# First layer of a twin-network kernel: tables on 48 partitions, early issues and bias bands from SyncE, shared modulation products

## The chip, the cores and the metric

One core of a Trainium2 chip. The metric is the device time of one execution in microseconds, the median of 3 runs. All arithmetic is in float32; large products are made of three passes on split operands (below).

## The reference, cut to what matters

Two networks run one after the other on a 512 x 1024 activation. The first has two layers, the second four. Only the first layer matters here: a modulation computed from a conditioning vector c, then a dilated-window attention with 18 heads in three groups, whose logits take a bias from a table of 32 buckets.

```
mod = silu(c) @ ada_w[i] + ada_b[i]               # 3 x 1024 values: shift, scale, gate
u = x * (1 + scale) + shift
q, k, v, gate = split(u @ w_in)                   # 18 heads of 64, groups with dilation 1, 4, 16
s = q k^T / 8 + bias_table[t5_bucket(offset)]     # only |offset| <= window / 2
o = softmax(s) v, weighted over the groups by softmax of log-sum-exp
y = (o * silu(gate)) @ w_out
x = layernorm(alpha * x + mod_gate * y)
```

The second network's third mixer is a differential attention with 4 heads that needs a bias table of its own (`rel_bias_2`) and a scalar lambda, from exponentials of two products of vectors.

## The kernel before

**Layout.** Activations are held transposed: 8 slices (KD) of 128 channels on partitions by 512 tokens. Weights come as a stream of chunks of 128 x 1024 (512 KB) through a ring of four slots, `w_raw`. Each chunk is split: ScalarE (ACT) copies it to `w_hi` in fp32r (`split_hi`, line 394, which waits for the landing and for the slot's last use by TensorE), GpSimd (POOL) makes `w_lo` as the difference (line 489), and SyncE (SP) loads the next chunk into a slot when `w_lo` of the old one is done (`four`, line 459). TensorE (PE) then makes each product in three matmuls (`product`, lines 401 to 403): hi x hi, hi x lo, lo x hi.

**Order.** Every engine has its program written out by hand; semaphores tie them. SP issues x slice 0, four chunks, seven x slices, and from then on only chunks, each behind its wait. ACT's queue issues everything else, in line with ACT's own work: the columns, the modulation blocks (`ada_ring`, four slots of 1 MB), the tables, the late rows (`late_ring`, three slots), the bias bands. A wait or a DMA issue on a sequencer holds all that is behind it there.

**Tables.** `hot` (67 rows x 3072) and `tab` (67 x 22) stand on 67 partitions: 32 buckets of the dilated bias, 3 rows for the windows' masks, 32 buckets of the second network's bias. PE multiplies them (lines 503 and 510), ACT copies the results to `bias_sb` (lines 1110 and 1117) and stores them to DRAM. From there `spread_a` (line 1155) writes 32 copies of each head's row to DRAM, six heads at a time, and `load_bands_a` (line 1163) reads skewed pieces back as `band_a`, 24 transfers for each of two heads. `bias_rows` (line 1234) are the same for the second network.

**Modulation.** For each of 8 steps t VectorE (DVE) sums the eight products of a 128 x 256 block with silu(c) (`ada_rows`, lines 1537 to 1548), PE sums over the partitions with a column of ones (line 553), DVE adds the base (line 1571) and forms the modulated slice `tmp` (line 1553), ACT rounds it to `u_hi` (line 1143), DVE subtracts to `u_lo` (line 1559). PE then runs the slice against the first four chunks (lines 556 to 565): 12 matmuls per slice. This is called the opening.

**Attention.** Three pairs of heads (jp = 0, 1, 2), two heads in each of three groups. Per pair: six projections q and k (`a_project`, line 567; in pair 0 the first four are the opening, and q and k of group 0 of the next pair are made in units 6 and 7 of the pair before), values (`a_values`, line 577), three gates, and eight units of scores, maxima, exp, turn and product. A projection is read by ACT (`a_parts`, line 1181: `qa_hi` or `ka_hi`) and DVE (line 1624: `qa_lo` or `ka_lo`). PE's values wait for all three `q_evac` of the pair. Pair jp uses 13 chunks: 6 for q and k, 4 for the values, 3 for the gates.

**Late rows.** The rest of the modulation (gate of layer one, all of layer two) is 32 rows of 128 x 1024, r = c // 8 the part: DVE takes two in each `a_parts` (line 1635, `late_rows`), ACT refills the ring in its own `a_parts`, ahead of the read of the projection (line 1185).

The waits of ACT in its `a_parts`:

```
chunk("a_in", at)
for c in (2 * e + 1, 2 * e + 2):
    if LATE_SLOTS <= c < LATE:
        act.wait_ge(late_used, c - LATE_SLOTS + 1)
        act.dma_start(late_ring[:, c % LATE_SLOTS, :], ada_late[c])
act.wait_ge(chunk_used, BASE["a_in"] + at + 1)
```

## Time and profile before

| | us |
|---|---|
| median of 3 runs | 3165.66 (3165.46 to 3169.13) |
| the profiled execution | 3166.86 |
| its span | 3165.1 |
| PE busy | 2855.0 (90%) |
| DVE busy | 1534.1 (48%) |
| POOL busy | 1123.4 (35%) |
| ACT busy | 917.7 (29%) |

DMA queue q1 (SP's) moved 241.20 MB, q10 (ACT's) 42.31 MB, of 285.14 MB in all. The profile lists for each instruction its start, its duration, and in brackets the idle time of its engine before it with what ended that. A name with a q behind it (ACTq, SPq) is the engine's own queue issuing; the time shown there is the time that the issues took, waits between them included. A matmul's duration reaches past the start of the next one, so the pace of a run of matmuls is read from the distance of starts. A float32 matmul shows as two passes (x4 for two calls), an fp32r one as one.

### The profile page before, as it was taken

The page shows a single profiled execution, that of the slowest core. Times are in us where ns is not written, and L with a number is a line of the kernel's source. Part 1 is how long each engine was busy: PE and PEld are TensorE (multiplying, and loading weights), DVE is VectorE, ACT ScalarE, POOL GpSimd, SP SyncE. Part 2 cuts the span into 40 slices and gives each one's busy share as a digit, 9 for nine tenths or more (in the row PEclk, how much of TensorE's full clock was granted, in tenths as well). Part 3 has the DMA queues.
Part 4 walks back from the last instruction along what each step waited for, and adds up shares of the span by engine and source line. Part 5 has one row for each costly group of instructions (what it writes and reads, how often), then busy time and mean ns, then how long its engine had stood idle before and what let it go on. Part 6 is the DMA issues. An engine that isn't in the chain of part 4 may idle for free.

```text
span 3165.1 us, 35456 instructions
## 1 busy us (share of the span) xinstructions
PE 2855.0 (90%) x13184; PEld 2325.8 (73%) x13184; DVE 1534.1 (48%) x2019; ACT 917.7 (29%) x1261; POOL 1123.4 (35%) x461
## 2 busy tenths in 40 slices
PE   1598897999899899997999988987999989899997
PEld 0487685878678688886788867875888868778885
DVE  2543435688666454305644125755644046464412
ACT  1132232455322322224322223333222231232222
POOL 1133222410234254441344433212544434434443
PEclk9899998999999999998999999998999999999998
DMA  5445321310122233332232322211333323223332
GB/s 194 123 162 160 99 64 60 100 34 21 60 73 88 65 106 99 98 102 85 75 98 93 103 83 72 72 41 54 109 97 100 100 69 98 93 73 94 99 100 87
DMA packets 106126, 285.14 MB, mean 90 GB/s; under 512 B 38658, under 2 KB 38786, under 8 KB 104664
## 3 DMA queue, kind: packets, MB, share of 16 engines
q1 hardware_dynamic: 67392, 241.20, 24.4%
q10 hardware_dynamic: 38619, 42.31, 4.4%
q8 instruction: 83, 1.36, 0.2%
q14 instruction: 32, 0.26, 0.0%
HBM read 281.22 MB, written 8.85 MB: 92 GB/s over the span
## 4 chain that ended last, share of the span: by engine, by line
issue 63%; POOL 23%; PE 11%; another core or an unknown queue 2%; POOLq 1%; DVE 1%; ACT 0%; ACTq 0%; DVEq 0%
POOL w_lo L489 23%; PE ps L401 4%; PE ps L402 4%; PE ps L403 4%; POOLq L488 0%; POOLq L162 0%; PE ps L503 0%; DVE x L1936 0%; DVE tmp L1930 0%; DVE rs L440 0%; ACT bias_sb L1110 0%; PE ps L432 0%; ACT w_hi L394 0%; DVE y L1979 0%
## 5 line engine op out<-in xcount | busy, mean ns | idle before, releaser
L489 POOL TENSOR_TENSOR w_lo<-w_raw,w_hi 128x1024 fp32r<-128x1024 f32 x452 | 1122.5, 2488 | 2027.2 <-ACT w_hi L394 2027.0
L401 PE MATMUL ps<-u_hi,w_hi 128*128 128x512 f32 x2240 | 909.8, 406 | 108.5 <-DVE u_lo L1768 58.2
L402 PE MATMUL ps<-u_lo,w_hi 128*128 128x512 f32 x2240 | 883.6, 394 | 0.0
L403 PE MATMUL ps<-u_hi,w_lo 128*128 128x512 f32 x2240 | 882.8, 394 | 0.0
L394 ACT ACTIVATE w_hi<-w_raw 128x1024 fp32r<-128x1024 f32 x452 | 474.2, 1054 | 869.6 <-PE ps L403 789.7
L401 PEld LDWEIGHTS ps<-u_hi,w_hi 128*128 128x128 f32 x2240 | 427.7, 191 | 220.4 <-DVE u_lo L1768 65.4
L402 PEld LDWEIGHTS ps<-u_lo,w_hi 128*128 128x128 f32 x2240 | 428.3, 191 | 99.0 <-issue 12.0
L403 PEld LDWEIGHTS ps<-u_hi,w_lo 128*128 128x128 f32 x2240 | 427.5, 191 | 90.9
L401 PE MATMUL ps<-h_hi,w_hi 128*128 128x512 f32 x704 | 278.1, 395 | 0.0
L403 PE MATMUL ps<-h_hi,w_lo 128*128 128x512 f32 x704 | 278.1, 395 | 0.0
L402 PE MATMUL ps<-h_lo,w_hi 128*128 128x512 f32 x704 | 278.1, 395 | 0.0
L1961 DVE TENSOR_TENSOR tmp<-ps,rs_x 128x512 f32<-128x512 f32 x88 | 60.8, 691 | 352.5 <-PE ps L403 352.5
L1979 DVE COPY y<-ps 128x512 f32<-128x512 f32 x32 | 22.1, 692 | 413.1 <-PE ps L403 413.1
L1598 DVE CAST h_hi<-tmp 128x512 f32 (+1 forms) x88 | 194.9, 2215 | 11.7 <-DVE tmp L1963 9.6
L1408 ACT ACTIVATE tmp<-tmp 128x512 f32<-128x512 f32 x88 | 55.6, 632 | 423.4 <-DVE tmp L1959 423.4
L403 PEld LDWEIGHTS ps<-h_hi,w_lo 128*128 128x128 f32 x704 | 132.0, 187 | 32.4
L401 PEld LDWEIGHTS ps<-h_hi,w_hi 128*128 128x128 f32 x704 | 132.0, 187 | 32.3
L402 PEld LDWEIGHTS ps<-h_lo,w_hi 128*128 128x128 f32 x704 | 132.0, 187 | 32.2
L401 PE MATMUL ps<-w_hi,u_hi 128*128 128x256 f32 (+1 forms) x256 | 82.5, 322 | 50.7 <-DVE qa_lo L1632 49.3
L401 PE MATMUL ps<-m_hi,w_hi 128*128 128x512 f32 x256 | 103.5, 404 | 12.1 <-DVE m_lo L2121 12.1
L402 PE MATMUL ps<-m_lo,w_hi 128*128 128x512 f32 x256 | 102.8, 402 | 0.0
L403 PE MATMUL ps<-m_hi,w_lo 128*128 128x512 f32 x256 | 102.6, 401 | 0.0
(262 smaller groups left out, 3312.8 us busy)
## 6 DMA issues: line engine op xcount, KB each, us to landing
w_raw<-in_stream SPq DMA_DIRECT2D x452, 512.0 KB, 3.5
late_ring<-in_ada_late ACTq DMA_DIRECT2D x32, 512.0 KB, 4.5
ada_ring<-in_ada ACTq DMA_DIRECT2D x8, 1024.0 KB, 7.6
dilated_bias_rows<-dilated_bias ACTq DMA_DIRECT2D x18, 244.1 KB, 5.1
band_a<-dilated_bias_rows ACTq DMA_DIRECT2D x96, 28.0 KB, 2.0
x<-in_x SPq DMA_DIRECT2D x8, 256.0 KB, 10.3
bias_rows<-bias_scratch ACTq DMA_DIRECT2D x4, 512.0 KB, 9.0
out_yT<-x SPq DMA_DIRECT2D x8, 256.0 KB, 2.0
```

The source lines that it names most:

```text
L394: nc.scalar.activation(w_hi[:, slot, :], w_raw[:, slot, :], ACT.Copy).then_inc(hi_ready, 1)
L401: nc.tensor.matmul(o, w[0], v[0], start=start, stop=False)
L402: nc.tensor.matmul(o, w[0], v[1], start=False, stop=False)
L403: return nc.tensor.matmul(o, w[1], v[0], start=False, stop=stop)
L489: nc.gpsimd.tensor_tensor(w_lo[:, s, :], w_raw[:, s, :], w_hi[:, s, :].bitcast(F32), ALU.subtract).then_inc(lo_ready, 1)
L1408: nc.scalar.activation(tmp[:, f, :], tmp[:, f, :], ACT.Silu).then_inc(g_silu, 1)
L1598: ch(nc.vector.tensor_copy(hi, src))
L1961: ch(nc.vector.tensor_tensor(tmp[:, 2 + f, :], bank(at + 1), rs_x[:, :], ALU.mult))
L1979: nc.vector.tensor_copy(y[:, m, :], bank(DOWN_BANKS[j])).then_inc(out_evac, 1)
```

## The change

- The tables stand on 48 partitions: the second network's buckets share rows 0 to 31 with the first's, in other columns.
- SP issues the modulation blocks, between the x slices, and the 48 band transfers of each pair, after rounds 3, 5 and 8 of four chunks. ACT's band and block issues go.
- Of the eight products per step DVE makes five; PE makes the other three as matmuls of the block itself with columns of silu(c), summed in PSUM with the column sum.
- In the opening ACT makes both the rounded and the plain modulated slice (`tmp`), from x, with scale and bias; DVE only subtracts.
- The second network's table and the lambda sum are multiplied after the opening, not before; the projections wait for their copies.
- ACT issues all 18 spreads after the opening; the copy of the second table and the exp for lambda come after them.
- The late rows: two at each `a_parts` except those of group 0 in the later pairs, four more ahead of the first maxima of each pair. ACT's refills stand behind the read of the projection, and behind the first two value chunks.

```diff
-BIAS_K = 32 + NG + 32
+BIAS_K = 48
+BANDS_AFTER = (3, 5, 8)
+ADA_PE = 3
@@ SP
+            def load_ada(t):
+                slot = t % ADA_SLOTS
+                if t >= ADA_SLOTS:
+                    sp.wait_ge(ada_turned, t - ADA_SLOTS + 1)
+                sp.dma_start(ada_ring[:, slot, :, :], ada_w[t]).then_inc(ada_landed[slot], 16)
+            def load_bands(jp):
+                sp.wait_ge(a_rows[jp], 16 * 2 * NG)
+                if jp:
+                    sp.wait_ge(m_ready, UNITS * jp)
+                for hh in range(2):
+                    for b in range(QB):
...
             load_x(0)
+            load_ada(0)
...
             four(0)
             for t in range(1, KD):
+                load_ada(t)
                 load_x(t)
-            with sp.Fori(1, N_CHUNKS // RING) as i:
+            done = 1
+            for jp in range(NJ):
+                with sp.Fori(done, BANDS_AFTER[jp]) as i:
+                    four(i)
+                done = BANDS_AFTER[jp]
+                load_bands(jp)
+            with sp.Fori(done, N_CHUNKS // RING) as i:
                 four(i)
@@ PE
-            pe.wait_ge(lam_prod, 1)
             pe.wait_ge(bias_copied, 1)
...
+            pe.wait_ge(c_silu, 1)
@@ PE, the opening
                 if t < KD:
+                    slot = t % ADA_SLOTS
+                    pe.wait_ge(ada_landed[slot], 16 * (t // ADA_SLOTS + 1))
                     pe.wait_ge(ada_used, t + 1)
                     for c in range(2):
-                        mm = pe.matmul(bank(7 - t % 2, 1, at=480 + c), ada_acc[:, t % 2, c * P:(c + 1) * P],
-                                       ones[:, 0:1], start=True, stop=True)
+                        w, o = slice(c * P, (c + 1) * P), bank(7 - t % 2, 1, at=480 + c)
+                        for k in range(KD - ADA_PE, KD):
+                            pe.matmul(o, ada_ring[:, slot, k, w], sc[:, k:k + 1], start=k == KD - ADA_PE, stop=False)
+                        mm = pe.matmul(o, ada_acc[:, t % 2, w], ones[:, 0:1], start=False, stop=True)
                     mm.then_inc(ada_turned, 1)
@@ PE, after the opening
+            pe.wait_ge(ada_turned, KD)
+            pe.wait_ge(lam_prod, 1)
+            for j in range(2):
+                at = A_BIAS_AT + j * S
+                mm = pe.matmul(bank(4 + j, p1=HC), tab[0:BIAS_K, HA:NB], hot[0:BIAS_K, at:at + S], start=True, stop=True)
+            mm.then_inc(bias_done, 1)
+            pe.matmul(bank(7, 2), ones[:, :], col[:, 16:18], start=True, stop=True).then_inc(lam_sum, 1)
@@ PE, a_project and a_values
-                    pe.wait_ge(ada_turned, KD)
+                    pe.wait_ge(bias_copied, 2)
...
+                pe.wait_ge(lam_exp, 1)
@@ ACT, the start: silu, split_hi(0), table copy, split_hi(1), split_hi(2); then
             begin("a_in")
             for t in range(KD):
-                if t + ADA_SLOTS < KD:
-                    act.wait_ge(ada_used, t + 1)
-                    act.dma_start(ada_ring[:, t, :, :], ada_w[t + ADA_SLOTS]).then_inc(ada_landed[t], 16)
-                act.wait_ge(u_tmp, n.up("u_tmp"))
-                nc.scalar.activation(u_hi[:, t, :], tmp[:, t % 2, :], ACT.Copy).then_inc(u_hi_ready, 1)
+                act.wait_ge(mod0_ready, t + 1)
+                act.wait_ge(x_landed[t], 16)
+                if t >= 2:
+                    act.wait_ge(u_ready, t - 1)
+                for dst in (u_hi[:, t, :], tmp[:, t % 2, :]):
+                    nc.scalar.activation(dst, x[:, t, :], ACT.Identity, scale=mod[:, 8 + t:9 + t],
+                                         bias=mod[:, t:t + 1]).then_inc(u_hi_ready, 1)
+                if t == 1:
+                    act.dma_start(a_bias_dram, bias_sb[0:HA, 0:A_BIAS]).then_inc(bias_stored, 16)
+                if t == 4:
+                    for c in range(LATE_SLOTS):
+                        act.dma_start(late_ring[:, c, :], ada_late[c]).then_inc(late_landed[c], 16)
+            act.wait_ge(bias_stored, 16)
+            for jp in range(NJ):
+                spread_a(jp)
+            act.wait_ge(bias_done, 2)
+            nc.scalar.activation(bias_sb[0:HC, A_BIAS_AT:], ...)
+            act.wait_ge(bias_copied, 2)
+            act.dma_start(bias_dram, bias_sb[0:HC, A_BIAS_AT:]).then_inc(bias_stored, 16)
+            act.wait_ge(lam_sum, 1)
+            nc.scalar.activation(col[:, 18:20], bank(7, 2), ACT.Exp).then_inc(lam_exp, 1)
@@ ACT, a_parts
-                for c in (2 * e + 1, 2 * e + 2):
...
                 ins.then_inc(a_hi_ready, 1)
+                if jp == 0 or g:
+                    late_refills(2)
+
+            def late_refills(count):
+                for _ in range(count):
+                    c = n.up("late")
+                    if c <= LATE - LATE_SLOTS:
+                        slot = (c - 1) % LATE_SLOTS
+                        act.wait_ge(late_used, c)
+                        act.dma_start(late_ring[:, slot, :], ada_late[c - 1 + LATE_SLOTS]).then_inc(late_landed[slot], 16)
@@ ACT, the pairs
-                    if g == 1:
-                        for hh in range(2):
-                            load_bands_a(jp, hh)
-                    if g == 2 and jp + 1 < NJ:
-                        spread_a(jp + 1)
                     if jp == 0 and g == 2:
+                        act.wait_ge(bias_stored, 32)
...
                 for c in range(QB):
                     chunk("a_in", A_CH * jp + 2 * NG + c)
+                    if c < 2:
+                        late_refills(2)
@@ DVE
-                for k in range(1, KD):
+                for k in range(1, KD - ADA_PE):
...
+            def first_lo(t):
+                dve.wait_ge(u_hi_ready, n.up("u_hi", 2))
+                nc.vector.tensor_tensor(u_lo[:, t, :], tmp[:, t % 2, :], u_hi[:, t, :].bitcast(F32),
+                                        ALU.subtract).then_inc(u_ready, 1)
...
-                    ch(nc.vector.tensor_tensor(pair, bank(7 - k % 2, 2, at=480), ada_base[:, :, k], ALU.add))
-                    dve.wait_ge(x_landed[k], 16)
-                    modulated(k, 0)
+                    nc.vector.tensor_tensor(pair, bank(7 - k % 2, 2, at=480), ada_base[:, :, k],
+                                            ALU.add).then_inc(mod0_ready, 1)
...
+                    if r >= 2:
+                        dve.wait_ge(late_turned, r - 1)
...
-                for c in (2 * e, 2 * e + 1):
+                if jp == 0 or g:
+                    more_rows(2)
...
+                more_rows(4)
                 if jp == 1:
                     late_mod(1)
                 a_maxima(i0)
```

## Rows read from the trace of the kernel before

**Rows 1.** The page, its first line.

```profile
span 3165.1 us, 35456 instructions
```

**Rows 2.** Windows: stretch, length, busy time of each engine, PE clock, DMA share, GB/s.

```profile
480.00:3165.00 2685.00, 2512.00 (x11424) 2035.60 (x11422) 1340.47 (x1648) 792.72 (x1082) 1010.07 (x408) 0.97 0.27 83
```

**Rows 3.** Time line of the start: start, duration, engine and line, what, idle before.

```profile
2.25 2.17 ACTq L1102 DMA_DIRECT2D hot<-in_onehot  x1
...
53.27 6.67 PE L503 MATMUL ps<-hot,tab 67*18 67x512 f32 x8 [53.27 <-DMA hot<-in_onehot]
...
59.98 1.79 ACT L1110 ACTIVATE bias_sb<-ps 18x1953 f32<-18x1953 f32 x1 [20.81 <-PE ps L503]
```

**Rows 4.** Windows of the first 53 us, while `hot` is on its way.

```profile
5.00:20.00 15.00, 0.00 (x0) 0.00 (x0) 0.68 (x3) 0.00 (x0) 0.00 (x0) 1.00 1.03 397
...
40.00:53.00 13.00, 0.00 (x0) 0.00 (x0) 3.05 (x7) 0.00 (x0) 0.00 (x0) 1.00 0.07 28
```

**Rows 5.** Time line of PE in the opening, first and second slice.

```profile
76.85 0.80 PE L401 MATMUL ps<-u_hi,w_hi 128*128 128x512 f32 x1 [9.14 <-DVE u_lo L1559]
...
82.14 0.85 PE L553 MATMUL ps<-ones,ada_acc 128*128 128x1 f32 x4
...
82.84 0.57 PE L401 MATMUL ps<-u_hi,w_hi 128*128 128x512 f32 x1
...
85.76 0.51 PE L553 MATMUL ps<-ones,ada_acc 128*128 128x1 f32 x4
```

**Rows 6.** Time line of DVE and ACT in the opening.

```profile
84.06 3.61 DVE L1546 SCALAR_TENSOR_TENSOR ada_acc<-ada_ring,sc,ada_acc 128x256 f32<-128x256 f32 x7
...
87.58 0.69 DVE L1559 TENSOR_TENSOR u_lo<-tmp,u_hi 128x512 fp32r<-128x512 f32 x1
...
94.12 0.63 ACT L1143 ACTIVATE u_hi<-tmp 128x512 fp32r<-128x512 f32 x1 [4.53 <-DVE tmp L1553]
```

**Rows 7.** Time line of PE: two of the four blocks of late columns.

```profile
179.67 1.95 PE L612 MATMUL ps<-ones,late_acc 128*128 128x1 f32 x16
...
412.66 2.25 PE L612 MATMUL ps<-ones,late_acc 128*128 128x1 f32 x16
```

**Rows 8.** Time line of PE: the opening's last matmul, and the four stalls.

```profile
112.33 0.39 PE L403 MATMUL ps<-u_hi,w_lo 128*128 128x512 f32 x1
...
127.03 0.80 PE L401 MATMUL ps<-u_hi,w_hi 128*128 128x512 f32 x1 [14.32 <-DVE qa_lo L1632]
...
158.34 0.69 PE L401 MATMUL ps<-w_hi,u_hi 128*128 128x384 f32 x1 [18.36 <-DVE qa_lo L1632]
...
277.72 0.69 PE L401 MATMUL ps<-w_hi,u_hi 128*128 128x384 f32 x1 [15.57 <-DVE qa_lo L1632]
...
392.01 0.69 PE L401 MATMUL ps<-w_hi,u_hi 128*128 128x384 f32 x1 [15.36 <-DVE qa_lo L1632]
```

**Rows 9.** Time line of ACT and DVE between the opening and the values.

```profile
110.34 3.17 ACTq L1161 DMA_DIRECT2D dilated_bias_rows<-dilated_bias  x5
...
119.31 0.60 ACT L1192 ACTIVATE ka_hi<-ps 128x512 fp32r<-128x512 f32 x1 [4.21 <-DVE late_acc L1610]
...
125.58 0.60 ACT L1194 ACTIVATE qa_hi<-ps 128x512 fp32r<-128x512 f32 x1 [4.73 <-DVE late_acc L1610]
...
133.20 2.60 DVE L1610 SCALAR_TENSOR_TENSOR late_acc<-late_ring,sc,late_acc 128x1024 f32<-128x1024 f32 x2
```

**Rows 10.** Time line of ACT: the first of pair 0's band issues, and ACT's next instruction.

```profile
131.92 2.15 ACTq L1173 DMA_DIRECT2D band_a<-dilated_bias_rows  x4
...
156.02 1.06 ACT L394 ACTIVATE w_hi<-w_raw 128x1024 fp32r<-128x1024 f32 x1 [23.52 <-issue]
```

**Rows 11.** The page, POOL's costliest group: line, count, busy, mean ns, idle before.

```profile
L489 POOL TENSOR_TENSOR w_lo<-w_raw,w_hi 128x1024 fp32r<-128x1024 f32 x452 | 1122.5, 2488 | 2027.2 <-ACT w_hi L394 2027.0
```

**Rows 12.** Time line of PE and DVE: pair 0's second scores, and its eighth maximum.

```profile
188.73 0.49 PE L401 MATMUL ps<-ka_hi,qa_hi 64*128 64x512 f32 x1
...
222.70 0.15 DVE L1661 TENSOR_REDUCE col<-col 128x1 f32<-128x2 f32 x1
```

More of the change, by code:

```diff
@@ L456, in load_x @@
                 sp.dma_start(x[:, t, :], xT[:, t, :]).then_inc(x_landed[t], 16)
+            def load_ada(t):
[9 more added lines that the diff above has]
+                    for b in range(QB):
+                        r = slice(32 * b, 32 * b + 32)
+                        for b2 in range(QB):
+                            at = (2 * jp + hh) * 32 * A_BIAS + (4 * (b2 - b) + 12) * SPAN + 31
+                            src = bass.AP(a_bias_rows.tensor, at, [[A_BIAS - 1, 32], [SPAN, 7], [1, 32]])
+                            dst = band_a[r, hh, 0:7 * P].rearrange("p (d c) -> p d c", d=7)[:, :, 32 * b2:32 * b2 + 32]
+                            sp.dma_start(dst, src).then_inc(band_landed, 16)
+                        for g in (1, 2):
+                            at = (HPG * g + 2 * jp + hh) * 32 * A_BIAS + (15 - 4 * b) * SPAN + 31
+                            src = bass.AP(a_bias_rows.tensor, at, [[A_BIAS - 1, 32], [4 * SPAN, QB], [1, 32]])
+                            w = slice((6 + g) * P, (7 + g) * P)
+                            dst = band_a[r, hh, w].rearrange("p (d c) -> p d c", d=QB)
+                            sp.dma_start(dst, src).then_inc(band_landed, 16)
             load_x(0)
+            load_ada(0)
             def four(i):
@@ L505, in _ @@
             mm.then_inc(bias_done, 1)
-            pe.wait_ge(lam_prod, 1)
             pe.wait_ge(bias_copied, 1)
-            for j in range(2):
-                at = A_BIAS_AT + j * S
-                mm = pe.matmul(bank(4 + j, p1=HC), tab[0:BIAS_K, HA:NB], hot[0:BIAS_K, at:at + S], start=True, stop=True)
-            mm.then_inc(bias_done, 1)
-            pe.matmul(bank(6, 2), ones[:, :], col[:, 16:18], start=True, stop=True).then_inc(lam_sum, 1)
+            pe.wait_ge(c_silu, 1)
             def turn(o, src):
@@ L1111, in _ @@
                                  ACT.Copy).then_inc(bias_copied, 1)
-            act.wait_ge(bias_copied, 1)
-            act.dma_start(a_bias_dram, bias_sb[0:HA, 0:A_BIAS]).then_inc(bias_stored, 16)
-            for c in range(RING - 1):
+            for c in range(1, RING - 1):
                 split_hi(act, c)
-            act.wait_ge(bias_done, 2)
-            nc.scalar.activation(bias_sb[0:HC, A_BIAS_AT:], ps[0:HC, 4:6, :].rearrange("p a b -> p (a b)"),
-                                 ACT.Copy).then_inc(bias_copied, 1)
             begun = set()
@@ L1161, in spread_a @@
                         act.dma_start(a_bias_rows[head], src).then_inc(a_rows[jp], 16)
[L1163 to L1179 removed]
+            begin("a_in")
@@ new lines, in _ @@
+            for t in range(KD):
+                act.wait_ge(mod0_ready, t + 1)
[10 more added lines that the diff above has]
+                        act.dma_start(late_ring[:, c, :], ada_late[c]).then_inc(late_landed[c], 16)
@@ L1565, in _ @@
                 if t >= 2:
-                    modulated_lo(t - 2)
+                    first_lo(t - 2)
                 if t:
@@ L1634, in a_parts, with more_rows @@
                                                    op1=ALU.subtract).then_inc(q_evac, 1)
-                for c in (2 * e, 2 * e + 1):
+                if jp == 0 or g:
+                    more_rows(2)
+            def more_rows(count):
+                for _ in range(count):
+                    c = n.up("late") - 1
                     if c < LATE:
@@ L2220, in _constants @@
     hot = np.zeros((BIAS_K, A_BIAS_AT + BIAS_W), np.float32)
-    hot[32 + NG + _buckets(delta, 128), A_BIAS_AT + np.arange(BIAS_W)] = 1.0
+    hot[_buckets(delta, 128), A_BIAS_AT + np.arange(BIAS_W)] = 1.0
     delta = ((np.arange(31) - 15)[:, None] + 16 * (np.arange(SPAN) - 31)[None, :]).reshape(-1)
@@ L2342 @@
         table[32 + g, g * HPG:(g + 1) * HPG] = 1.0
-    table[32 + NG:, HA:] = a["rel_bias_2"]
+    table[0:32, HA:] = a["rel_bias_2"]
     hot, rope, inv, windows = _constants()
```

46 lines of the change are left out of this document (9 added, 37 removed).

## The prediction

> **What bounds the kernel now.** I read the page first, then the windows by stage, then what TensorE (PE) waits for, and last the time lines of the engines before each of its waits. The span is 3165.1 us [rows 1]. From 480 us on PE is busy 2512 of 2685 us and the change touches nothing there [rows 2]; so all of it is decided in the first layer, before 480 us, where PE's idle time is a delay of everything behind it.
>
> At the start PE's first matmul waits 53.27 us for the table `hot`, issued at 2.25 us [rows 3]. Look at the transfers meanwhile: 397 GB/s from 5 to 20 us, but 28 GB/s at a DMA share of 0.07 from 40 to 53 us, about one engine of sixteen [rows 4]. Then the table's matmuls take 6.67 us and their copy 1.79 us [rows 3], and the opening (8 slices of the modulated input, 12 matmuls each) begins at 76.85 us [rows 5] and ends at 112.33 + 0.39 = 112.7 us [rows 8]. A slice comes every 4.53 + 0.63 = 5.16 us, paced by VectorE's eight products [rows 6].
>
> After it PE stands still four times [rows 8]: 14.32 us to 127.03, 18.36 to 158.34, 15.57 to 277.72, 15.36 to 392.01. All four end with `qa_lo`. The first is the pace of the units of ScalarE (ACT) and VectorE, 125.58 - 119.31 = 6.27 us each, ACT waiting for late rows [rows 9]. The other three are 48 band transfers that ACT issues in front of its own work, 131.92 to 156.0 us, 23.52 us of idle ACT, so 0.5 us each [rows 10].
>
> **The change, part by part.** All times are made against the profiled run, 3166.9 us, 1.2 above the median of 3165.7.
>
> *Tables on 48 partitions.* The row shows one engine's rate for 67 partitions [rows 4]. At 397 GB/s the table's 0.59 MB share the engines with 1.25 MB of x and first modulation block; both are in after about 1.9/0.397 = 5 us plus 2 to 4 us of start: `hot` at 7.5, the block at 9. The bound on the other side is no gain in engines (rival 2). The Trainium skill, DMA: Bandwidth & Descriptors, section Why a DMA increments its semaphore by 16 and not by 1, has a transfer use the largest number of engines up to 16 that divides its outer sizes: 1 for 67, 16 for 48. By that rule the forecast stands, without it rival 2.
>
> *Start.* Table matmuls 7.5 to 14.2, copy to 16.0 [rows 3]. ACT's silu no longer stands behind its ring issues. On SP the blocks go ahead: x0, block 0, four chunks, then three pairs of block and x, 7 MB, in by about 22 us at 397 GB/s. Column sums of slice 0 at 16.1, 16 small matmuls where there were 4: 0.85 x 4 = 3.4 us at the low clock [rows 5], so to 19.8. The first modulated slice needs VectorE's pair, two ACT passes and a subtraction, and PE must do columns 1: its 12 matmuls start about 23.5. w_lo of the first chunks (2.49 us each on POOL, [rows 11]) is ready about 24, so it just follows.
>
> *Opening.* VectorE per slice: five products instead of eight, 3.61/7 = 0.52 each, so 1.5 us less, and the modulating pass goes to ACT: about 3.3 us. ACT does two passes of 0.63 [rows 6]; the form with scale and bias from columns is not in the trace, bounded by 0.6 and 1.0 us (and a table load once), covered by the 4.9 below either way. PE per slice: 82.84 to 85.76 = 2.9 us for 12 matmuls at 2.4 GHz [rows 5], plus 16 small ones, 1.95 us [rows 7]: 4.9 us. PE becomes the bound, and the slice is hardly shorter than 5.16. So sharing the products gives little by itself. First slice at 1.2 GHz 76.85 to 82.14 = 5.3 us [rows 5]: 23.5 + 5.3 = 28.8; then 6 x 1.95 + 7 x 2.9 = 32; one fall of the clock as in this opening, 2 us: end at 63. Blocks 4 to 7 wait on SP for sums that are one slice old; 1 MB needs 3 to 5 us, hidden by four slots. **Gain 112.7 - 63 = 49.7.**
>
> *From the opening to the values.* Here something is added: after its last slice (59) ACT issues 18 spreads instead of 6, 3.17/5 = 0.63 each [rows 9] = 11.3, to 70.5; copy of the second table, table load and exp about 2.5 together (an estimate from the 1.79 of the first copy [rows 3]): 73. These 18 move 4.4 MB; if the queue holds ACT up they cost up to 20 instead of 11. Only then come the units that let PE go on, and PE's second table (four matmuls where the first took eight) hides beneath. A unit is now split 1.05, high part 0.6, low part 0.7 [rows 6, 9], two late rows 2.60 [rows 9], an issue 0.35: 5.3; the refills are issued before the split, so the landing is nearly covered (6.27 if not: +1 per unit). `qa_lo` of the second group comes at 73 + 12 = 85, where it came 14.3 after the opening and now comes 22: ACT's burst costs 8 here. Two projections of 13 us together (127.03 to 140.0 [rows 8]): values start at 98. With bands off ACT the next `qa_lo` is there by 96. Before: 158.34 - 112.7 = 45.6; now 35. **Gain 10.4.**
>
> *Bands on SP, pair 0.* SP issues 48 bands at 0.5 us once chunk 11 is issued (chunk 7 split, about 97): 97 to 121. Queued behind: chunk 12, landed about 125, and ACT waits for it in order before it copies the values, 127. PE has work: values to 118, scores, late columns 1.95 and a gate projection until 128.4 (158.34 to 188.73 is 30.4 [rows 8, 12]). So it hides, with 1 to 2 us to spare. The values lose the restart at the low clock: **gain 1.9**, a small wait for chunk 9 kept.
>
> *Pair 1.* SP waits for the eighth maximum (222.7 in old time [rows 12]), issues to 247, chunk 20 lands 251; ACT wants it at about 256, after the projection before the last. The stall of 15.57 goes, and 1.7 of restart (384-column matmuls at 0.17). **Gain 17.3.** *Pair 2.* The same, 392.01 - 277.72 = 114.3 later and a little more: bands 339 to 363, chunk 32 at 367. ACT wants it three projections of 5.4 before 376.65, at 361. ACT is 6 us late, its unit by 3, and PE is still in the projection before. Next late is nothing. **Gain 15.36 + 2.4 = 17.8.** The two halves of the late rows moved out of units 6 and 7, and the four extra before the maxima, lie under some 18 us of values: nothing, and if that cover went, 4 x 1.3.
>
> Sum: 49.7 + 10.4 + 1.9 + 17.3 + 17.8 = 97.1; 3166.9 - 97.1 = **3070 us**, 3.0% less. Its own range is 3058 to 3084: below, no fall of the clock and shorter waits in the first 20 us; above, units of 6.27 (+3), spreads held up (+9).
>
> **Rival 1: the opening runs at 1.2 GHz.** Of four blocks of 16 small matmuls one runs 2.25 us and ahead of slow matmuls, the one at 179.67 not [rows 7]; every slice now has such a block. For it: the clock was low for the first slice. Against: gaps now nearly vanish, and the fast slices before had gaps of 2 us. Price: 6 x 3.4 + 7 x 5.3 = 57.5 for 32 + 2, so +23: 3093. The Trainium skill, TensorE: Matmul & The Clock Gate, section What's actually happening, says that "activity releases the throttle"; by it this rival hangs on whether single-column matmuls are activity, which no row settles.
>
> **Rival 2: the table's transfer stays on one engine.** 0.59 MB at 28 GB/s is 21 us, beside that engine's sixteenth of 8 MB, 18 us: `hot` at 40. The opening slides by 32 less the 2 to 3 waited for blocks: +30, 3100.
>
> **Rival 3, slower: SP chokes on the bands.** SP carries all weights, and each pass of 48 stands before a chunk. If SP gets them off only as they land (2 us instead of 0.5), each pass is 96 us, PE starves three times: 3 x 48 x 1.5 = 216, less 10 of slack, 3276. It decides above 0.5 + (97 + 10)/144 = 1.24 us per issue. Against it: ACT issued the same shapes at 0.5 [rows 10], and nothing makes SP's issue dearer. A weak form, some us per pass beyond the slack of pair 0, gives 3084 to 3110.
>
> **Numbers.** Forecast 0.69, rival 1 0.13, rival 2 0.06, weak rival 3 0.06, rival 3 0.03, better than 3056 0.03. The range of 3056 to 3101 leaves out rival 3, half of rival 2, the end of its weak form and the better case, a little over 0.1. A difference under 0.2% cannot be told from none here; faster by more 0.96, within 0.01, slower 0.03.
>
> **What would show it.** Right: first matmul at 7 to 9 us; opening to 60 to 66 with PE nearly without gaps; ACT's queue 11 us in spreads; PE idle about 22 us after the opening, none of 15 or more afterwards; SP's bands in three runs of 24 us. Wrong: matmuls 0.43 apart all through the opening (rival 1), a first matmul after 30 us (rival 2), chunk splits that wait for landing for tens of us (rival 3), or ACT held for 20 us by the spreads.

## The result, and the profile after

The change takes the kernel from 3166.11 to 3087.61 us (medians of four runs each, the latter from 3087.26 to 3089.77), a ratio of 0.9752 with the interval 0.9735 to 0.9769: 2.5% faster. The profiled execution took 3089.77 us where that of before took 3166.86, its span 3088.0 against 3165.1, so 77.1 us went, where 97.1 were forecast.

First the page's first lines, and the window behind the first layer. Its columns are those of [rows 2].

```profile
span 3088.0 us, 35641 instructions
...
PE 2861.1 (93%) x13280; PEld 2335.5 (76%) x13280; DVE 1512.2 (49%) x1987; ACT 924.0 (30%) x1269; POOL 1121.7 (36%) x461
```

```profile
480.00:3088.00 2608.00, 2455.95 (x11219) 1996.94 (x11218) 1298.17 (x1588) 773.12 (x1057) 992.25 (x400) 0.97 0.27 83
```

PE is busy 94% of that stretch, as before. A sharper mark of where the change ends is the last of the 18 units' maxima (the reduction whose pair 0 rows stand in [rows 12]). It came at 457.26 us before and comes at 380.52 now, 76.7 earlier, and from it to the end it is 2707.8 us before and 2707.5 after. All of the gain lies ahead of that mark.

Now what PE waits for, its time line with the columns of [rows 3] and [rows 8]:

```profile
12.15 6.66 PE L540 MATMUL ps<-hot,tab 48*18 48x512 f32 x8 [12.15 <-DMA hot<-in_onehot]
...
31.17 0.80 PE L404 MATMUL ps<-u_hi,w_hi 128*128 128x512 f32 x1 [3.48 <-DVE u_lo L1591]
...
66.33 0.39 PE L406 MATMUL ps<-u_hi,w_lo 128*128 128x512 f32 x1
...
88.27 0.80 PE L404 MATMUL ps<-u_hi,w_hi 128*128 128x512 f32 x1 [19.44 <-DVE qa_lo L1671]
...
100.96 0.44 PE L404 MATMUL ps<-w_hi,u_hi 128*128 128x384 f32 x1
...
117.30 0.44 PE L404 MATMUL ps<-w_hi,u_hi 128*128 128x384 f32 x1 [3.57 <-POOL w_lo L526]
...
142.93 0.79 PE L404 MATMUL ps<-ka_hi,qa_hi 64*128 64x512 f32 x1 [10.68 <-ACT va L1274]
...
317.56 0.45 PE L404 MATMUL ps<-w_hi,u_hi 128*128 128x384 f32 x1 [0.60 <-DVE qa_lo L1671]
```

The 53.27 us of waiting for `hot` [rows 3] are 12.15 now, and the opening ends at 66.7 us instead of 112.7. Of the four stalls of [rows 8] the first is longer (19.44 where it was 14.32) and the other three are gone: in pair 2 only 0.60 us is left of 15.36. But pair 0 has two waits that it had not: 3.57 us for `w_lo` and **10.68 us for `va`**, the copy of the values by ACT. Stretch by stretch:

| stretch | before | after | gain | forecast |
|---|---|---|---|---|
| start to end of the opening | 112.7 | 66.7 | 46.0 | 49.7 |
| to the first values of pair 0 | 45.6 | 34.2 | 11.4 | 10.4 |
| to pair 0's second scores | 30.4 | 42.0 | -11.6 | 1.9 |
| to the second maximum, and on to the eighth | 34.0 | 36.9 | -3.0 | 0 |
| to pair 1's first maximum | 75.6 | 58.25 | 17.35 | 17.3 |
| to the last maximum | 159.0 | 142.4 | 16.6 | 17.8 |

(The eighth maximum stands at 179.87 us, pair 1's first at 238.12; before at 222.70 and 298.30.) Two thirds of the miss, 13.5 of 20 us, are one line of the table, the values of pair 0; the opening has 3.7 and the stretch behind the second scores 3.0. What ran on the other engines then? The queue of SP, and ACT:

```profile
102.87 1.80 SPq L479 DMA_DIRECT2D band_a<-dilated_bias_rows  x4
...
117.04 3.94 SPq L485 DMA_DIRECT2D band_a<-dilated_bias_rows  x2
121.03 4.38 SPq L479 DMA_DIRECT2D band_a<-dilated_bias_rows  x4
...
137.85 20.72 SPq L389 DMA_DIRECT2D w_raw<-in_stream  x8
```

```profile
62.60 10.23 ACTq L1179 DMA_DIRECT2D dilated_bias_rows<-dilated_bias  x16
...
110.84 2.74 ACTq L1264 DMA_DIRECT2D bias_rows<-bias_scratch  x4
...
118.36 7.97 ACTq L1230 DMA_DIRECT2D late_ring<-in_ada_late  x2
...
141.45 1.06 ACT L397 ACTIVATE w_hi<-w_raw 128x1024 fp32r<-128x1024 f32 x1 [13.96 <-DMA w_raw<-in_stream]
```

The 48 bands begin at 102.87 us and the chunk behind them is issued at 137.85: 35 us and not 24, because four of them take 4.38 us, or two 3.94, where the first four took 1.80. ACT then waits 13.96 us for that chunk, and in its program order the copy of the values stands behind it. The windows say what happened in between (columns as in [rows 2], the last two the DMA share and GB/s):

```profile
102.00:113.00 11.00, 11.00 (x65) 11.00 (x64) 7.53 (x6) 1.54 (x2) 2.55 (x2) 1.00 0.98 232
113.00:128.00 15.00, 11.43 (x60) 10.41 (x59) 4.79 (x4) 3.18 (x3) 6.18 (x3) 0.89 1.02 305
128.00:138.00 10.00, 4.25 (x19) 3.19 (x17) 0.00 (x0) 0.00 (x0) 1.96 (x1) 0.89 0.51 92
```

The DMA engines are full up to 128 us. At 110.84 ACT hands out four `bias_rows` spreads of 512 KB, and late rows of the same size on top. The queues from 113 to 128 us (packets, MB, share of the 16 engines' time; q10 is ACT's, q1 SP's) show two things: ACT's queue has four fifths of the engines, and the bands, in pieces of 128 bytes, ask for more engine time than their bytes tell (19.0% for 0.34 MB against 82.8% for 4.24):

```profile
q10 hardware_dynamic: 1163, 4.24, 82.8%
q1 hardware_dynamic: 2909, 0.34, 19.0%
```

SP's issues, which wait for no semaphore within a pass, slow down (from 105.68 to 108.68, at a share of 1.06, they had not: four in 1.90 us, two in 1.02); and VectorE gets its late rows late, so that ACT's two refills at 118.36 span 7.97 us where they span 1.65 elsewhere:

```profile
124.68 1.28 DVE L1649 SCALAR_TENSOR_TENSOR late_acc<-late_ring,sc,late_acc 128x1024 f32<-128x1024 f32 x1 [6.35 <-DMA late_ring<-in_ada_late]
```

### The profile page after: what moved, and what is told of

Its sections match the earlier page's. It is cut to its first block, busy times and chain, and to the rows that moved or that the text cites. A ratio compares the mean times of both kernels' runs of the same rounds, so it can differ in the third digit from the quotient of the medians.

```text
span 3088.0 us, 35641 instructions
## 1 busy us (share of the span) xinstructions
PE 2861.1 (93%) x13280; PEld 2335.5 (76%) x13280; DVE 1512.2 (49%) x1987; ACT 924.0 (30%) x1269; POOL 1121.7 (36%) x461
## 4 chain that ended last, share of the span: by engine, by line
issue 64%; POOL 23%; PE 11%; POOLq 1%; DVE 1%; DMA 0%; ACT 0%; ACTq 0%; DVEq 0%
POOL w_lo L526 23%; PE ps L404 4%; PE ps L405 4%; PE ps L406 4%; DMA hot<-in_onehot 0%; POOLq L525 0%; POOLq L164 0%; PE ps L540 0%; DVE x L1981 0%; DVE tmp L1975 0%; DVE rs L443 0%; PE ps L435 0%; ACT w_hi L397 0%; DVE acc L2026 0%; DVE y L2024 0%
## 5 line engine op out<-in xcount | busy, mean ns | idle before, releaser
L1635 DVE CAST h_hi<-tmp 128x512 f32 (+1 forms) x88 | 196.0, 2228 | 10.6 <-DVE tmp L2008 8.6
L1636 DVE TENSOR_TENSOR h_lo<-tmp,h_hi 128x512 f32 (+1 forms) x88 | 85.8, 975 | 8.7
```

Source lines behind the costliest of these rows:

```text
L1635: ch(nc.vector.tensor_copy(hi, src))
L1636: nc.vector.tensor_tensor(lo, src, hi.bitcast(F32), ALU.subtract).then_inc(signal, 1)
```

## The experiments

Two questions had to be told apart: which parts of the change carry the 77 us, and what took back the missing 20. My theory for the second was the queue: pair 0's bands start late and run slowly, and chunk 12 waits behind them. The rivals were the burst of spreads, the late rows, and the opening itself. Each run is read by its profiled span (after: 3088.0), its ratio to the kernel before with a 95% interval, and its last maximum (after: 380.52). The last two come from one execution each, the profiled one. From the last maximum to the end it is 2709.4 to 2710.5 us in all the experiments, but 2707.5 in the changed kernel, so a gain read from the last maximum is 2 to 3 us too large against it; the difference of the spans is the more careful number.

**The `bias_rows` spreads later.** The four transfers move from pair 0 to pair 1.

```diff
-                    if jp == 0 and g == 2:
+                    if jp == 1 and g == 2:
                         act.wait_ge(bias_stored, 32)
```

> The changed kernel with the four bias_rows transfers (2 MB, for the second network) issued in pair 1 instead of pair 0. Theory (the band issues of pair 0 on SP were held from 108 to 131 us because the DMA engines were full with these rows and the late rows, share 1.0): the 48 issues take 24 to 27 us instead of 35, chunk 12 lands near 131 instead of 141, the wait of 10.7 us falls to about 2 and the 3.6 for chunk 9 to about 1; 3087.6 less 11 = 3076 to 3079. Rival (SP's issues are just late and slow, whatever else moves): the 10.7 stays above 7, 3084 to 3087.

Measured: 3088.99 us, ratio 0.9748 (0.9732 to 0.9765), span 3087.4. The bands go in 26 us, and the wait for `va` is a third of what it was:

```profile
102.53 1.80 SPq L479 DMA_DIRECT2D band_a<-dilated_bias_rows  x4
...
129.01 2.10 SPq L389 DMA_DIRECT2D w_raw<-in_stream  x4
```

```profile
134.12 0.50 PE L404 MATMUL ps<-ka_hi,qa_hi 64*128 64x512 f32 x1 [3.29 <-ACT va L1274]
...
234.07 3.54 PE L657 MATMUL ps<-ones,late_acc 128*128 128x1 f32 x16 [4.01 <-DVE col L1661]
```

The second maximum comes at 139.26, 8.8 us earlier. So the spreads beside them are what stretched the bands. It is not that the engines are full: here, too, their share is 1.04 from 111 to 114 us and 1.07 to 117, and from 112.77 on four bands take 2.12 us, two 1.29, four 1.90. What differs from 113 to 128 us is how the two queues divide the engines:

```profile
q10 hardware_dynamic: 655, 2.35, 51.3%
q1 hardware_dynamic: 6336, 0.75, 36.6%
```

But the last maximum is only 2.7 earlier and the time the same as before this edit, where 3076 to 3079 were expected: in pair 1 the same spreads now stand ahead of late rows (VectorE waits 7.17 us for one to land) and PE waits 4.01 us there, where it had not. The cost was moved more than removed.

**The same spreads one at a time**, in the loop over pair 0's six heads (u = 1 to 4), behind the bands.

```diff
+                    if jp == 0 and 1 <= u < 5:
+                        head = u - 1
+                        act.wait_ge(bias_stored, 32)
+                        src = bass.AP(bias_dram.tensor, head * BIAS_W, [[0, P], [1, BIAS_W]])
+                        act.dma_start(bias_rows[head], src).then_inc(c_rows, 16)
```

> The changed kernel with the four bias_rows transfers issued one at a time in units 1 to 4 of pair 0, where ACT has slack and the DMA engines are nearly idle. Theory (the first trial with them in pair 1 removed 8.8 us in pair 0 and lost 6 in pair 1, because there they stood among ACT's refills again): the gain of about 9 in pair 0 stays; last maximum at 371 to 373 instead of 380.5, 3078 to 3081. Rival (2 MB of rows cost their time wherever they go): last maximum above 376.

Measured: 3080.82 us (3078.57 to 3080.92), 0.972 (0.9703 to 0.9736), span 3079.0. Bands in 27 us, from 101.85; the stall for `w_lo` falls to 0.20 and that for `va` to 7.65; last maximum 369.54, 11.0 earlier (9.0 by the spans). The DMA share in the same window is as high as in the changed kernel (1.02 there), which says once more that the share alone does not slow SP:

```profile
113.00:128.00 15.00, 13.88 (x76) 11.80 (x74) 4.63 (x4) 2.12 (x2) 5.68 (x3) 1.00 1.03 201
```

The four spreads are issued at 154.45 to 165.55 us, 3.7 us apart, and here the gain stays: pair 0 keeps 8.2 us at its second maximum (139.87), and pair 1 does not lose it again.

**The bands one round of four chunks earlier.**

```diff
-BANDS_AFTER = (3, 5, 8)
+BANDS_AFTER = (2, 5, 8)
```

> The changed kernel with pair 0's bands after round 2 of the chunks instead of 3 and pair 1's after 5 stays. Theory (the 10.7 us wait is chunk 12 queued behind 48 band issues): bands run from about 70 to 95 us, before the values need a chunk from SP; the 10.7 us wait goes, the 3.6 stays; 3076 to 3079. Rival (the same place in line only moves the loss, now chunk 8 is behind the bands and the spreads' 4.4 MB hold their issue): a new wait of some us inside the values, 3082 to 3090.

Measured: 3081.24 us, 0.9729 (0.9713 to 0.9746), span 3077.4. SP issues the bands from 70.21 to about 98, and the next chunk right behind:

```profile
70.21 2.13 SPq L479 DMA_DIRECT2D band_a<-dilated_bias_rows  x4
...
98.74 3.92 SPq L389 DMA_DIRECT2D w_raw<-in_stream  x4
```

```profile
119.52 0.69 PE L404 MATMUL ps<-w_hi,u_hi 128*128 128x384 f32 x1 [4.74 <-POOL w_lo L526]
```

No wait for `va` is left; a wait of 4.74 us for `w_lo` takes part of the place. Last maximum 367.39, 13.1 earlier (10.6 by the spans; the median is 2 us above the 3076 to 3079 expected, with that new wait). With the two runs above, this shows the cause: the bands' place and their pace in SP's queue make the 10.68 us, and mending either shortens it or takes it away.

**Tables back on 67 partitions**, all else as changed.

```diff
-BIAS_K = 48
+BIAS_K = 67
```

(with the rows of the two tables at their old places)

> The changed kernel with the tables back on 67 partitions, all else as changed. Theory (the early table is all from its 48 partitions: 67 run on one engine at 28 GB/s, 0.82 MB = 29 us, beside that engine's sixteenth of 7.75 MB, 17 us): first matmul at 45 to 50 us instead of 12, the opening ends about 31 later (blocks have landed by then), 3087.6 + 31 = 3112 to 3124. Rival (it is early because ACT's and SP's queues are ordered otherwise): first matmul before 30, under 3105.

Measured: 3135.74 us, 0.9904 (0.9888 to 0.9921), span 3131.7, last maximum 421.23.

```profile
55.65 5.28 PE L540 MATMUL ps<-hot,tab 67*18 67x512 f32 x6 [55.65 <-DMA hot<-in_onehot]
```

```profile
40.00:55.00 15.00, 0.00 (x0) 0.00 (x0) 0.00 (x0) 0.00 (x0) 0.00 (x0) 1.00 0.06 26
```

By the spans 43.7 of the 77.1 us hang on the partition count alone (48 by the medians), more than the 24 to 36 expected, and the window shows the one engine's 26 GB/s again, which had been 28 in [rows 4]. The Trainium skill (DMA: Bandwidth & Descriptors, section Why a DMA increments its semaphore by 16 and not by 1) has a transfer use the largest count of engines up to 16 that divides its outer sizes; the trace agrees for 67, where 26 GB/s go at a DMA share of 0.06, one sixteenth. For 48 it shows only that it is more than one: 0.59 MB land in 10.3 us, which is 57 GB/s, beside other loads.

**All eight products on VectorE.**

```diff
-ADA_PE = 3
+ADA_PE = 0
```

> The changed kernel with all eight products on VectorE and the 12 small matmuls per slice gone. Theory (sharing shortens a slice only from about 5.0, VectorE's pace, to 4.53, PE's pace): slices of 5.0, first slice about 2 later; opening 3 to 6 us longer, 3091 to 3094. Rival (the sharing gives nothing, the two paces are equal): within 1.5 of 3087.6.

Measured: 3092.63 us (3089.73 to 3095.04), 0.9766 (0.975 to 0.9782), span 3087.9.

```profile
53.58 0.50 PE L404 MATMUL ps<-u_hi,w_hi 128*128 128x512 f32 x1 [1.22 <-DVE u_lo L1591]
```

PE now waits 1.22 us per slice for VectorE, and yet a slice takes 4.58 us against 4.53: the products taken off PE just leave the gap. PE resumes after the opening at 88.64 against 88.27, so in the profiled executions sharing the products is worth 0.4 us; that of this run is its fastest, and its median is 5 us above that of the changed kernel, with intervals that overlap. The 3091 to 3094 expected came by that median, the slices of 5.0 us that it was worked out from did not. What had brought the slice from 5.16 to 4.58 is the modulating pass taken off VectorE, 0.55 us at 83.22 in the kernel before.

**The bands alone, on the kernel before.** SP issues them as in the change, nothing else is touched.

```diff
-                    if g == 1:
-                        for hh in range(2):
-                            load_bands_a(jp, hh)
...
+            for jp in range(NJ):
+                with sp.Fori(done, BANDS_AFTER[jp]) as i:
+                    four(i)
+                done = BANDS_AFTER[jp]
+                load_bands(jp)
```

> The kernel before with only the band transfers moved to SP, after rounds 3, 5 and 8. Theory (of the three stalls of 15 to 18 us all go, and pair 0 gives part back by chunk 12 waiting behind the bands): pairs 1 and 2 gain 34, pair 0 gains 18 less 5 to 11; 3166 less 41 to 48 = 3118 to 3125, and the eighth maximum of pair 0 comes 7 to 14 earlier than before. Rival (SP's own work suffers more than ACT gains): less than 34 in all, above 3132.

Measured: 3124.95 us, 0.9868 (0.9851 to 0.9884), span 3117.3, last maximum 407.77, so 49.5 us from this edit in the profiled execution, which is the fastest of its four; by the ratio it is 42. Expected were 41 to 48. Here, too, pair 0's bands take 31 us (137.85 to 168.67), but PE waits only 2.33 us for `va` and 1.86 for `w_lo`.

**Bands and tables alone**, on the kernel before.

```diff
-BIAS_K = 32 + NG + 32
+BIAS_K = 48
```

(and the bands as in the run above)

> The kernel before with two edits alone: the band transfers on SP, and the tables on 48 partitions. Theory (these two carry the change; the sharing, ACT's modulating and the 18 spreads in one go give nothing or cost): the tables take the same 43 to 44 us off bands alone, the last maximum of the dilated layer comes at 362 to 370 us, earlier than the 380.5 of the whole change; about 3074 to 3084. Rival (the early products on SP, ACT's modulating and the sharing are needed to use an early table, since the blocks are then the next wait): the last maximum at 378 or later, 3086 or more.

Measured: 3084.04 us (3081.52 to 3088.05), 0.9736 (0.972 to 0.9753), span 3079.7, last maximum 370.16.

```profile
14.60 6.67 PE L530 MATMUL ps<-hot,tab 48*18 48x512 f32 x8 [14.60 <-DMA hot<-in_onehot]
...
87.58 0.79 PE L402 MATMUL ps<-u_hi,w_hi 128*128 128x512 f32 x1 [14.32 <-DVE qa_lo L1656]
...
115.33 0.44 PE L402 MATMUL ps<-w_hi,u_hi 128*128 128x384 f32 x1 [1.40 <-POOL w_lo L516]
...
135.04 0.79 PE L402 MATMUL ps<-ka_hi,qa_hi 64*128 64x512 f32 x1 [4.67 <-ACT va L1266]
```

This is the run that says most. The last maximum moves by 49.5 with the bands, by 37.6 more with the tables, and then **back by 10.4 with all the rest of the change** (370.16 to 380.52). How much of that is real is less sure: the spans differ by 8.3, but they set this run's fastest execution against the changed kernel's slowest; the medians, 3084.04 and 3087.61, differ by 3.6, and the intervals overlap. What can be said is that the rest of the change brings nothing on top of these two edits, and may cost some us. The rest makes the opening end 6.5 us earlier (66.7, here 87.58 - 14.32 = 73.3), but PE resumes at 88.27, not at 87.58: 18 spreads ahead of the first unit, where here there are 6, take it back. From there to the second scores it is 54.7 us instead of 47.5.

**Six spreads after the opening**, the other twelve two at a time in the loop over pair 0's heads.

```diff
-            for jp in range(NJ):
-                spread_a(jp)
+            spread_a(0)
...
+                    if jp == 0 and u < 3:
+                        for i in (2 * u, 2 * u + 1):
+                            spread_one(1, i)
```

(u from 3 to 5 likewise for pair 2)

> The changed kernel with only pair 0's 6 spreads issued in one go after the opening, the 12 others two at a time in the units of pair 0. Theory (ACT's 18 issues, 10.2 us after its last slice, stand on the path): first qa_hi at 68 instead of 75.6, PE's wait of 19.4 us falls to 12, everything behind it comes 7 earlier; 3080 to 3082. Rival (the pace is set by late rows and chunk landings): the wait falls, but comes back in the units or the values, 3085 to 3088.

Measured: 3087.05 us, 0.9742 (0.9726 to 0.9759), span 3087.4. PE's wait is 15.12 instead of 19.44, but the last maximum comes only 3.5 earlier and the span 0.6, with 8.22 us for `va` still there: the 3080 to 3082 expected did not come, and the rival's "the wait falls, but comes back" did.

**Late rows after the projections.** None in the first two units of pair 0 (its first group), eight instead of four ahead of its maxima.

```diff
-                if jp == 0 or g:
+                if g or (jp == 0 and False):
                     more_rows(2)
...
-                more_rows(4)
+                more_rows(8 if jp == 0 else 4)
```

(the refills likewise)

> The changed kernel with no late rows in the first two units of pair 0 and eight instead of four ahead of its first maxima (refills moved alike). Theory (a unit takes 6.35 us because its two late rows take 3.6, not 2.6, one of them standing against POOL's w_lo, and ACT waits for both): the first two units take about 3 each, PE's wait of 19.4 falls to 13, and about 6 us are gained if the rows fit under the values; 3081 to 3083. Rival (the rows and their 2 MB are only moved to where the bands and chunk 12 wait): 3086 to 3092.

Measured: 3084.08 us, 0.9738 (0.9722 to 0.9755), span 3079.2. PE's wait after the opening is 10.99 instead of 19.44 (it resumes at 78.84, 9.4 earlier), and the last maximum comes 11.4 earlier (8.8 by the spans, 3.5 by the medians), with 8.50 us for `va` still there. The late rows in the first units hold PE more than the burst does: 8.45 us for them, 4.3 for twelve of the spreads.

**`w_lo` cut short on POOL.** For the first four chunks POOL makes 256 of the 1024 columns, the rest is zero.

```diff
+                w = 256 if is_first(i) else CW
...
-                    nc.gpsimd.tensor_tensor(w_lo[:, s, :], w_raw[:, s, :], w_hi[:, s, :].bitcast(F32),
+                    nc.gpsimd.tensor_tensor(w_lo[:, s, 0:w], w_raw[:, s, 0:w], w_hi[:, s, 0:w].bitcast(F32),
```

> The changed kernel, but POOL makes only 256 of the 1024 columns of w_lo for the first four chunks; the rest is set to zero at the start (this part of the low products is left out). POOL's four instructions then take 0.6 us each instead of 2.4. Theory (VectorE's products of slice 2, 6.1 us for 2.4 of work, stand still while POOL runs, an exclusive port): they take 2.4 to 3.5, the first opening matmul comes at 27.5 to 29 instead of 31.2, the whole 2 to 4 us earlier. Rival (they are slowed by the blocks that land at a DMA share of 0.98 in the same stretch): still about 6 us, first matmul at 31.

Measured: 3084.97 us (3083.94 to 3085.72), 0.9734 (0.9718 to 0.975), span 3083.9. The same instructions of VectorE, and the window around them, first in the changed kernel:

```profile
24.39 2.08 DVE L1576 TENSOR_SCALAR ada_acc<-ada_ring,sc 128x256 f32<-128x256 f32 x1
26.51 4.01 DVE L1578 SCALAR_TENSOR_TENSOR ada_acc<-ada_ring,sc,ada_acc 128x256 f32<-128x256 f32 x4
```

```profile
24.40:31.00 6.60, 3.29 (x16) 3.20 (x15) 6.46 (x7) 1.52 (x2) 4.27 (x2) 1.00 0.98 350
```

and then with the short `w_lo`:

```profile
24.38 0.35 DVE L1581 TENSOR_SCALAR ada_acc<-ada_ring,sc 128x256 f32<-128x256 f32 x1
24.77 2.05 DVE L1583 SCALAR_TENSOR_TENSOR ada_acc<-ada_ring,sc,ada_acc 128x256 f32<-128x256 f32 x4
```

```profile
24.40:31.00 6.60, 6.60 (x24) 5.92 (x24) 5.85 (x14) 3.04 (x4) 0.00 (x0) 1.00 0.99 338
```

The DMA share is the same (0.98 and 0.99); POOL's 4.27 us in this window are gone, and VectorE's 2.08 is 0.35, its 4.01 is 2.05. So it is POOL and not memory traffic that makes VectorE slow. The opening's first matmul comes at 27.54 instead of 31.17, PE resumes at 84.41, 3.9 earlier, and the last maximum at 373.81 (the span is 4.1 shorter, the median 2.6). The Trainium skill (SBUF — State Buffer, section SBUF: two separate sides) says that VectorE and GpSimd share a pair of ports under an exclusive lock, which some of VectorE's instructions need, among them those with two SBUF inputs, and that the engine that comes second is blocked fully; the trace agrees: 1.73 us more on one instruction, and of the four products in 4.01 us one took 2.45 and the others 0.49.

**All moved.** Bands early, few late rows, six spreads, and `bias_rows` one per head: the four edits above together.

> The changed kernel with four moves at once: pair 0's bands after round 2, no late rows in the first two units, 6 spreads after the opening with the rest in the units of pair 0, bias_rows one at a time in units 1 to 4 of pair 0. Theory (each loss has its own cause): PE's wait after the opening falls from 19.4 to about 7, the wait of 10.7 goes, some 5 us remain in the values for chunk 8 behind the bands; 15 to 23 us less than the changed kernel, about 3065 to 3073. Rival (the moves hit the same queue again): no better than the bands moved alone, 3078 or more.

Measured: 3071.57 us (3070.8 to 3072.44), 0.9697 (0.9681 to 0.9713), span 3069.8. PE's wait after the opening is 6.68 (it resumes at 74.63), 4.75 for `w_lo` and 3.65 for `va`; last maximum 359.9. By the spans the four edits taken one by one gave 10.6, 8.8, 0.6 and 9.0, together 29; the four at once give 18.2. They partly shorten the same waits (the 10.68 us for `va` are there only once). The medians are too coarse to show it: 6.4, 3.5, 0.6 and 6.8, together 17, for 16 at once.

**And pair 0's six spreads in the opening**, one per slice from the third on.

```diff
-            act.wait_ge(bias_stored, 16)
-            spread_a(0)
...
+                if t >= 2:
+                    if t == 2:
+                        act.wait_ge(bias_stored, 16)
+                    spread_one(0, t - 2)
```

> The kernel with four moves, with a fifth: pair 0's six spreads are issued one per slice in the opening, while ACT waits 3 us per slice, so SP's bands can start about 12 us earlier and be done before the values need a chunk. Theory: PE's wait after the opening falls from 6.7 to about 3, the wait of 4.75 in the values to below 1.5; the last maximum comes 6 to 8 earlier than 359.9; 3063 to 3067. Rival (the bands then compete with chunks 4 to 7 and the late rows, or ACT's slices get longer): no gain, 3070 or more.

Measured: **3067.24 us** (3065.22 to 3069.47), 0.9677 (0.9661 to 0.9693), span 3067.7, last maximum 358.28, the best of all: 20.4 us under the changed kernel, 3.2% under the one of before. It is 4.3 us ahead of the run above by the medians and 1.6 by the last maximum, where 6 to 8 were expected. The last of pair 0's spreads is issued at 61.18, the bands start at 64.20, and PE's wait after the opening, expected at 3, is unchanged:

```profile
75.30 0.79 PE L404 MATMUL ps<-u_hi,w_hi 128*128 128x512 f32 x1 [6.67 <-DVE qa_lo L1679]
...
121.27 0.46 PE L404 MATMUL ps<-ka_hi,qa_hi 64*128 64x512 f32 x1 [2.78 <-ACT va L1271]
```

Spreads after the opening were thus no longer what held PE in the run before; in its 6.67 us ACT has the copy of the second table, the table load and the first units.

## Why the prediction was right, and where it was not

The measured 3087.6 lies in the range of 3056 to 3101, 17.6 us above the forecast of 3070 and above the 3058 to 3084 that the sum gave itself; of the mechanisms forecast all but one came. That one, pair 0's bands, had been foreseen only as a weak form of rival 3, with a chance of 0.06.

*The table.* Right in kind: 48 partitions take more than one engine, rival 2 did not come. The sizes were off in both directions. `hot` landed at 12.15 and not at 7.5; what it shared the engines with beyond the x and the first block that the sum counted, no run separates. The price of one engine was put at 30 us and measured 43.7: rival 2 had it for 0.59 MB, landing at 40, and the 67 partitions are 0.82 MB and landed at 55.65.

*The opening.* Forecast from 23.5 to 63, measured 31.17 to 66.7. The first matmul is 7.7 late: 4.6 from `hot`, and the rest from the lock of VectorE by POOL (3.6 in the run with the short `w_lo`). The trace of before had shown such slow products of VectorE beside `w_lo`, seven in 5.57 us where [rows 6] has 3.61, and I had read past them:

```profile
70.63 5.57 DVE L1546 SCALAR_TENSOR_TENSOR ada_acc<-ada_ring,sc,ada_acc 128x256 f32<-128x256 f32 x7
```

Then 4.0 us were given back: a slice took 4.53 instead of the 4.9 forecast, and the one fall of the clock, priced at 2, did not come. That the opening ends only 3.7 late is errors that partly cancel, and luck. "PE becomes the bound, and the slice is hardly shorter than 5.16. So sharing the products gives little by itself" is right in its second sentence (0.4 us).

*Rival 1* did not come. In the changed kernel, too, only the first slice runs with matmuls 0.43 us apart, which is 512 columns at 1.2 GHz, and the others with 0.23, the pace of 2.4 GHz. The second slice from 38.30 on is already fast, right behind a block of 16 single-column matmuls:

```profile
36.03 0.63 PE L406 MATMUL ps<-u_hi,w_lo 128*128 128x512 f32 x1
36.46 0.86 PE L589 MATMUL ps<-sc,ada_ring 128*128 128x1 f32 x6
...
38.62 0.40 PE L405 MATMUL ps<-u_lo,w_hi 128*128 128x512 f32 x1
38.85 0.40 PE L406 MATMUL ps<-u_hi,w_lo 128*128 128x512 f32 x1
```

So such blocks, one in every slice, did not bring the clock down. What they do by themselves no run here settles.

*After the opening.* The burst was 16 spreads in 10.23 us and two more, as the 11.3 forecast; the first unit's `qa_hi` came at 75.59 for 73, PE's wait ended at 88.27 for 85. A unit takes 6.36 us (93.20 - 86.84), not 5.3: the upper value that the prediction named for uncovered landings, but for another reason. Two late rows take 3.63 us while POOL splits, where [rows 9] had 2.60. That row was a pair with POOL at rest; in the two units ahead of it the kernel before had shown 4.56 and 4.59, so the term was taken from the wrong row:

```profile
88.14 3.63 DVE L1649 SCALAR_TENSOR_TENSOR late_acc<-late_ring,sc,late_acc 128x1024 f32<-128x1024 f32 x2
```

```profile
120.61 4.56 DVE L1610 SCALAR_TENSOR_TENSOR late_acc<-late_ring,sc,late_acc 128x1024 f32<-128x1024 f32 x2
```

(The first is the changed kernel, the second the one before.) The sum's gain of 10.4 for this stretch is 10.6 by its own terms, 45.6 less 35, and 11.4 was measured.

*Pair 0's bands.* This is the step that failed: "SP issues 48 bands at 0.5 us once chunk 11 is issued (chunk 7 split, about 97): 97 to 121", and from it "it hides, with 1 to 2 us to spare", **gain 1.9**. They ran from 102.87 to 137.85, 6 us late from the opening and the slower units, and 11 longer. The stretch cost 11.6 us instead of gaining 1.9, a mis-sizing of 13.5 us and two thirds of the 20 missing; 3.0 more went up to the eighth maximum. The 0.5 us per issue from [rows 10] was a price with the DMA engines to spare: from 140 to 156 us their share was 0.37 to 0.40. I had looked whether the SP queue was late, not what ACT's `bias_rows` and late rows, pushed up beside it, would take of the engines that both share. That the queue is the cause, and not something else in the stretch, is shown by another place of the bands and by another time of the spreads, in pair 1 or one by one. Why an issue of SP gets slower beside them is not shown: not by the DMA share alone, which was as high where the bands kept their pace. It is the weak form of rival 3, in pair 0 alone.

*Pairs 1 and 2* were right to 1.2 us: 17.35 for 17.3, and 16.6 for 17.8. No row had been given for the 2.4 in the latter; with 0.60 us of the stall of 15.36 left, 1.8 of it came. There the bands meet engines with room (DMA share 0.35 from 180 to 204 us): four in 1.80 us at 180.10, as at 102.87.

*The passes on ACT* took 0.81 us each, within 0.6 to 1.0, and lay covered.

*The range.* It reached to 3101 for the rivals and not for this; the sum's own bounds end at 3084, and the result is inside the range only through what was added for the rivals, of which the weak form of rival 3, with 3084 to 3110, is the one that came.

What stays open: whether the rest of the change costs anything on top of bands and tables (8.3 us in the profiled executions, 3.6 by the medians), and how it splits between late rows, burst and `bias_rows`, was not measured edit by edit on that base; the edits on the changed kernel overlap, as the sum of 29 for 18.2 shows.

## What to carry to other kernels

When issues move to another queue, ask not only what they stand in front of there, but what the other queue has under way on the shared engines at that time: an issue of 0.45 us took 1.1 to 2 beside four spreads and the late rows, and every load behind it came late. A transfer that runs at the rate of one engine can cost more than all finer edits (here 43.7 us for 67 partitions instead of 48): look for it first. And test the parts of a large change one by one: here two of them gave as much as the whole.

## What was unexpected of the hardware

- **SP's issues slow down while ACT's queue has most of the DMA engines.** With 82.8% of the engines' time for ACT's queue and 19.0% for SP's, two bands took 3.94 us and four 4.38 on SP (0.92 and 1.80 with room), though nothing in the program makes one band wait for the one before. With 51.3% and 36.6% they kept nearly their pace, at a share that was at times as high (1.07). ACT's four `bias_rows` issues took 2.74 us just before, 0.69 each, so its queue was hardly held.
- **POOL blocks VectorE all at once, not in part.** A product of 128x256 takes 0.35 us free and 2.08 while a `w_lo` of 2.4 us runs, with the same DMA share; 4 of them 2.05 and 4.01. Not every instruction is held: `qa_lo`, which reads PSUM, takes its usual 0.69 us at 87.53, while a `w_lo` runs from 87.01 to 89.37.
- **ACT's pass with scale and bias from columns** takes 0.81 us for 128x512, against 0.63 for a plain copy of the same size [rows 6].
- **The pace can be low while the granted clock reads 1.00.** From 31.17 to 36.5 us the opening's matmuls are 0.43 us apart, and the window there still shows 1.00; before a clock is argued from that column, the distance of the matmuls is to be read beside it:

```profile
33.00:35.00 2.00, 2.00 (x6) 1.57 (x5) 1.09 (x3) 0.00 (x0) 0.00 (x0) 1.00 0.01 4
```
